# Hybrid decoder trunk: inputs laid out on the host, squares summed on VectorE, a feed-forward entry of four tiles

## The reference

```python
def _rmsnorm(x, g):
    y = xf * lax.rsqrt(jnp.mean(xf * xf, axis=-1, keepdims=True) + NORM_EPS)
    return (y * g.astype(F32)).astype(x.dtype)

def _hybrid_layer(h, ...):
    hn = _rmsnorm(h, g_mix_pre) * valid
    u = (hn @ w_in).astype(F32)                       # 7704 columns, split into the branches
    y_sb, y_gla, y_ml, y_ret = ...                    # stick-breaking, GLA, mLSTM, retention
    gates = jax.nn.sigmoid(merge_logits + b_merge)
    merged = sum(gates[n] * (branches[n] @ w_branch[n]))
    h = h + _rmsnorm(merged @ w_out, g_mix_post)
    f = _rmsnorm(h, g_ffn_pre)
    ffn_out = (jax.nn.silu(f @ ffn_w_gate) * (f @ ffn_w_up)) @ ffn_w_down
    return h + _rmsnorm(ffn_out, g_ffn_post)
```

## Time and profile before

| | us |
|---|---|
| median of 3 runs (lowest, highest) | 961.67 (961.19, 963.05) |
| the profiled execution | 962.09 |
| its span | 959.2 |
| TensorE busy | 947.6 |
| TensorE weight loads busy | 897.3 |
| VectorE busy | 600.6 |
| ScalarE busy | 515.2 |
| GpSimd busy | 80.0 |

### The profile page before, as it was taken

One profiled execution on the slowest core, in us unless ns is written; L12 is line 12 of the kernel. 1 busy time (PEld: TensorE's weight loads), 2 busy tenths in 40 slices (PEclk: granted clock), 3 DMA queues, 4 the chain that ended last, 5 costly groups with the idle time before them and its releaser, 6 DMA issues.

```text
span 959.2 us, 18955 instructions
## 1 busy us (share of the span) xinstructions
PE 947.6 (99%) x7398; PEld 897.3 (94%) x7398; DVE 600.6 (63%) x924; ACT 515.2 (54%) x825; POOL 80.0 (8%) x72
## 2 busy tenths in 40 slices
PE   9999999999999999999999999999999999999998
PEld 7999988899999999999989998988999899999886
DVE  6776675467956655553467775763678666655543
ACT  6645654475466544444456447544854765454442
POOL 1000000000031222210100000000000322221000
PEclk9999999999999999999999999999999999999999
DMA  7585445356553655555545653454564546556652
GB/s 218 171 249 184 147 146 170 124 141 168 174 178 105 196 173 170 172 180 165 166 140 147 211 156 126 134 161 133 141 184 160 176 132 213 181 175 205 211 180 84
DMA packets 165563, 159.41 MB, mean 166 GB/s; under 512 B 9835, under 2 KB 157790, under 8 KB 165502
## 3 DMA queue, kind: packets, MB, share of 16 engines
q1 hardware_dynamic: 163806, 155.17, 52.5%
q10 hardware_dynamic: 1504, 3.33, 1.1%
q0 software_dynamic: 192, 0.07, 0.0%
HBM read 156.37 MB, written 1.06 MB: 164 GB/s over the span
## 4 chain that ended last, share of the span: by engine, by line
PE 94%; DVE 2%; DMA 2%; ACT 1%; SPq 1%; issue 0%; DVEq 0%; ACTq 0%
PE banks L710 25%; PE banks L712 25%; PE banks L711 25%; PE banks L1111 2%; PE banks L1113 2%; PE banks L1112 2%; PE banks L747 2%; PE banks L744 1%; PE banks L743 1%; PE banks L762 1%; DMA raw<-in_w_in 1%; PE banks L976 1%; ACT hi L1195 1%; DVE lo L1610 1%; DMA raw<-in_ffn_w_up 1%; PE banks L974 1%
## 5 line engine op out<-in xcount | busy, mean ns | idle before, releaser
L1610 DVE TENSOR_TENSOR lo<-raw,hi 128x1024 fp32r<-128x1024 f32 (+1 forms) x287 | 347.9, 1216 | 144.9 <-ACT hi L1195 144.3
L710 PE MATMUL banks<-xh,hi 128*128 128x272 f32 (+1 forms) x1456 | 420.1, 289 | 0.2 <-issue 0.2
L712 PE MATMUL banks<-xh,lo 128*128 128x272 f32 (+1 forms) x1456 | 416.3, 286 | 0.0
L711 PE MATMUL banks<-xl,hi 128*128 128x272 f32 (+1 forms) x1456 | 415.0, 285 | 0.0
L1195 ACT ACTIVATE hi<-raw 128x1024 fp32r<-128x1024 f32 (+1 forms) x287 | 300.1, 1048 | 138.5 <-PE banks L712 43.7
L710 PEld LDWEIGHTS banks<-xh,hi 128*128 128x128 f32 x1456 | 274.4, 188 | 6.1 <-issue 4.3
L712 PEld LDWEIGHTS banks<-xh,lo 128*128 128x128 f32 x1456 | 274.5, 189 | 0.0
L711 PEld LDWEIGHTS banks<-xl,hi 128*128 128x128 f32 x1456 | 274.1, 188 | 0.0
L1301 ACT ACTIVATE gates<-banks,par 128x272 f32<-128x272 f32 (+1 forms) x64 | 30.8, 481 | 93.8 <-PE banks L712 91.0
L2114 POOL TENSOR_TENSOR silu_g<-silu_g,rstd 128x272 f32<-128x272 f32 (+1 forms) x44 | 54.5, 1238 | 214.9 <-ACT silu_g L1491 214.9
L2107 POOL TENSOR_TENSOR sq<-sq 128x272 f32<-128x272 f32 (+1 forms) x18 | 21.8, 1213 | 593.0 <-ACT sq L1464 592.1
(11 more groups left out here) (277 smaller groups left out, 1416.1 us busy)
## 6 DMA issues: line engine op xcount, KB each, us to landing
raw<-in_w_in SPq DMA_DIRECT2D x54, 1024.0 KB, 5.3
raw<-in_ffn_w_gate SPq DMA_DIRECT2D x22, 1024.0 KB, 5.3
raw<-in_ffn_w_up SPq DMA_DIRECT2D x22, 1024.0 KB, 5.3
raw<-in_ffn_w_down SPq DMA_DIRECT2D x19, 1024.0 KB, 5.1
raw<-in_w_out SPq DMA_DIRECT2D x8, 1024.0 KB, 5.2
raw<-in_w_in SPq DMA_DIRECT2D x12, 512.0 KB, 4.3
raw<-in_w_branch SPq DMA_DIRECT2D x12, 512.0 KB, 5.5
raw<-in_ffn_w_down SPq DMA_DIRECT2D x4, 768.0 KB, 4.3
```

Source lines behind the costliest of these rows:

```text
L710: mm(dst, wh, mh, start=start, stop=False)
L711: mm(dst, wh, ml, start=False, stop=False)
L712: return mm(dst, wl, mh, start=False, stop=stop)
L1610: tt(half_of(lo, g, c), half_of(raw, g, c), half_of(hi, g, c).bitcast(F32), ALU.subtract).then_inc(lo_ready, 2 if g in G_MIX else 1)
```

## The change

The host now lays out the tokens as `hT` wants them, all parameters as one [128, 2, 88] block, the small group as [128, 8, 128] and the gate weights padded. The transposes, their evictions and the first squares go. Norms 0 and 2 add their squared tiles on VectorE, 8 to 4 to 2, and TensorE takes two. Before the two kinds of boundary (feed-forward entries, entry of layer 1) VectorE makes hi and lo of halves 2 and 3. `together` does all high and low-weight passes of a k step for its tiles before the ones with the low part of x. The feed-forward starts four tiles; layer 1's entry has three tiles in step, and its mean square stands between mqk1's halves.

```diff
-WARM_START, WARM_NORM = 5, 4
-RING, NORM_BANK = (0, 1, 2, 3), 5
+WARM_START, WARM_NORM = 8, 4
+RING, NORM_BANK, INPUT_NORM_BANK = (0, 1, 2, 3), 5, 6
...
-FIRST_LAGS = ((0, KT), (0, 0, 3))
+SUMS = ({0: 2, 1: KT - 2, 2: 2, 3: KT - 2}, {0: 2, 1: KT - 2, 2: 2})
...
+OUT_FIRST, FFN_FIRST, FFN_LATE = 3, 4, 4
+FIRST_ORDER = in_step((0, KT)), [[(n, k) for n in range(3)] for k in range(KT)]
+FFN_ORDER = [[(n, k) for n in range(FFN_FIRST - int(k >= FFN_LATE))] for k in range(KT - 1)]
+FFN_ORDER += [[(n, KT - 1)] for n in range(FFN_FIRST - 1)] + [[(FFN_FIRST - 1, k)] for k in range(FFN_LATE, KT)]
...
 SP:
-            sp.dma_start(xt[0:META, 0, :], meta_tokens).then_inc(meta_loaded, 16)
             for n in range(2):
-                sp.dma_start(xt[:, 1:3, n * 512:n * 512 + 512],
-                             x[0].rearrange("(b p) n -> p b n", p=P)[:, :, n * 512:n * 512 + 512]).then_inc(x_loaded[n], 16)
-            load_rows(sp, PARAM_ROWS[4:7], par_loaded)
+                sp.dma_start(hT[:, 4 * n:4 * n + 4, :], tokens[:, 4 * n:4 * n + 4, :]).then_inc(x_loaded[n], 16)
...
-                        load(g, cols(w_in[l], C_CODE, 32))
-                        sp.dma_start(raw[g % 2][:, :, 32:64], cols(w_in[l], C_MI, 32)).then_inc(small_loaded, 16)
-                        sp.dma_start(raw[g % 2][:, :, 64:128], cols(w_in[l], C_MF, 64)).then_inc(small_loaded, 16)
+                        load(g, w_small[l])
 TensorE, together:
+                for step in steps:
+                    for n, k in step:
+                        ...
+                        if k > high:
+                            high_ready(k)
+                        mm(dst, wh[:, k, f], mh[:, k, q0:], start=k == 0, stop=False)
+                        mm(dst, wl[:, k, f], mh[:, k, q0:], start=False, stop=False)
+                    for n, k in step:
+                        ...
+                        if k > low:
+                            low_ready(k)
+                        last = mm(ps[:, 0:T - q0], wh[:, k, half_cols(g, c)], ml[:, k, q0:], start=False, stop=k == KT - 1)
 TensorE, mean_square:
+                left = (0, KT - 1) if n % 2 else (0, 1)
+                pe.wait_ge(sq_summed[l], sums_before(l, n) + SUMS[l][n])
+                pe.wait_ge(sq_ready[l][n], KT)
+                for k in left:
+                    last = mm(ps[:, 0:T - q0], cut["mean"], sq[:, k, q0:], start=k == 0, stop=k == left[1])
 TensorE, first:
-                    mean_square_first()
                     small_first(t)
-                    together([(t + 1, g + 1, 0), (t + 2, g + 1, 1)], in_step(FIRST_LAGS[l]), uh, ul, 0, *ready)
+                    together([(t + 1, g + 1, 0), (t + 2, g + 1, 1)], FIRST_ORDER[l], uh, ul, 0, *ready)
+                    pe.wait_ge(first_loaded, 16)
+                    mean_square(l, 0, 0)
                 else:
-                    together([(t, g, 0), (t + 1, g + 1, 0), (t + 2, g + 1, 1)], in_step(FIRST_LAGS[l]), uh, ul, 0, *ready,
-                             mean_square(l, 0, 0))
+                    together([(t, g, 0), (t + 1, g + 1, 0), (t + 2, g + 1, 1)], FIRST_ORDER[l], uh, ul, 0, *ready)
 TensorE, group:
+                    if l and name == "mqk1" and j == 0:
+                        mean_square(l, 0, 0)
 TensorE, gate_up:
-                together([(t, g, 0), (t + 1, g, 1), (t + 2, g + 1, 0)], in_step((0, 0, 0)), xh, xl, q0,
-                         lambda k: pe.wait_ge(xh_ready[l], 2 * KT + k + 1), lambda k: pe.wait_ge(xl_ready[l], 2 * KT + k + 1),
-                         mean_square(l, 2, q0))
-                features(t + 3, g + 1, 1, xh, xl, q0)
+                together([(t + n, g + n // 2, n % 2) for n in range(FFN_FIRST)], FFN_ORDER, xh, xl, q0,
+                         lambda k: pe.wait_ge(xh_ready[l], 2 * KT + k + 1), lambda k: pe.wait_ge(xl_ready[l], 2 * KT + k + 1))
+                mean_square(l, 2, q0)
 TensorE, start: the 24 transposes of x and the 2 of the parameters are taken out
 ScalarE, first / output / gate_up / down:
-                for j in range(2):
-                    round_half(half + 2 + j)
+                if l == 0:
+                    for j in range(2):
+                        round_half(half + 2 + j)
...
-                round_half(2 * G_OUT[l] + KT - 2 + ROUND_AHEAD)
                 square_sublayer(l, 1, t + KT - 1, KT - 1, q0)
...
                 for c in range(2):
-                    if c:
-                        round_half(n + 1)
                     gate_tile(c, t + c)
+                round_half(n + 3)
                 for c in range(2):
                     up_tile(c, t + 2 + c, c)
-                    round_half(n + 2 + c)
...
-                        if 2 * j + c < 2 * NDOWN - 1:
+                        if 2 * j + c < 2 * NDOWN - 2:
 ScalarE, order:
+            act.dma_start(par[:], parameters).then_inc(par_loaded, 16)
             act.dma_start(const[:, 0:PIECE_AT[1]], consts[:, 0:PIECE_AT[1]]).then_inc(first_loaded, 16)
...
-                    square_first()
-                    act.wait_ge(bias_loaded, 48)
-                    diagonals()
                     for k in range(KT):
                         round_in(l, k)
-                        if k == 3:
+                    for k in range(KT):
+                        if k == 2:
                             round_half(2)
                             round_half(3)
-                    root(l, 0, 0)
+                        square_h(l, 0, k, 0)
                     round_half(4)
                     round_half(5)
+                    act.wait_ge(first_loaded, 16)
+                    root(l, 0, 0)
                 else:
                     half = 2 * G_MIX[l] + ROUND_AHEAD
-                    round_half(half - 1)
                     for k in range(KT):
                         round_in(l, k)
                         if k == 2:
+                            act.wait_ge(hi_ready, half)
                             round_half(half)
-                    round_half(half + 1)
+                    for n in range(1, 4):
+                        round_half(half + n)
                     root(l, 0, 0)
...
                 root(l, 1, q0)
-                round_half(2 * G_GU[l] - 1 + ROUND_AHEAD)
                 round_ffn_x(l, q0)
-                round_half(2 * G_GU[l] + ROUND_AHEAD)
+                act.wait_ge(hi_ready, 2 * G_GU[l] + ROUND_AHEAD)
+                for n in range(2):
+                    round_half(2 * G_GU[l] + ROUND_AHEAD + n)
                 root(l, 2, q0)
+                round_half(2 * G_GU[l] + ROUND_AHEAD + 2)
 VectorE:
+            def round_and_rest(n):
+                g, c = n // 2, n % 2
+                dve.wait_ge(hi_ready, n)
+                dve.wait_ge(raw_loaded[g % 2], 16 * (g // 2 + 1))
+                dve.wait_ge(half_used, n - 3)
+                nc.vector.tensor_copy(half_of(hi, g, c), half_of(raw, g, c)).then_inc(hi_ready, 1)
+                rest_of_half(n)
+
+            def sum_squares(l, n, q0):
+                ...
+                dve.wait_ge(sq_ready[l][n], KT)
+                tt(sq[:, 0:4, q0:], sq[:, 0:4, q0:], sq[:, 4:8, q0:], ALU.add).then_inc(sq_summed[l], 1)
+                dve.wait_ge(sq_summed[l], done + 1)
+                tt(sq[:, 0:2, q0:], sq[:, 0:2, q0:], sq[:, 2:4, q0:], ALU.add).then_inc(sq_summed[l], 1)
...
 VectorE, rest_of_in and rest_of_ffn_x: no lo inside the k loop any more
 VectorE, first:
+                if l:
+                    pads(l)
+                    rest_of_half(2 * g + REST_AHEAD + 3)
                 dve.wait_ge(rstd_ready[l], 1)
...
 VectorE, gate_up:
+                for ahead in (1, 2):
+                    rest_of_half(n + ahead)
                 dve.wait_ge(rstd_ready[l], 3)
...
                 gate_tile(0, t)
-                rest_of_half(n + 1)
                 gate_tile(1, t + 1)
+                rest_of_half(n + 3)
                 for c in range(2):
                     up_tile(c, t + 2 + c)
-                    rest_of_half(n + 2 + c)
                     rest_of_prod(c, slice(c, c + 1), c + 1)
 VectorE, order:
+            for k in range(2):
                 rest_of_in(0, k)
             scale_small(0, hi_ready)
             scale_small(1, lo_ready)
+            for k in range(2, KT):
+                rest_of_in(0, k)
             rest_of_half(2)
             rest_of_half(3)
+            sum_squares(0, 0, 0)
             for l in range(DEPTH):
                 for n in range(2):
                     rest_of_half(2 * G_MIX[l] + ROUND_AHEAD + n)
+                    if l and n == 0:
+                        sum_squares(l, 0, 0)
                 run_steps(l, parts)
                 output(l)
+                for n in (2, 3):
+                    round_and_rest(2 * G_GU[l] + n)
                 add_sublayer(l, 1, q0, rest_of_ffn_x(l, q0))
+                sum_squares(l, 2, q0)
                 gate_up(l)
                 if l < DEPTH - 1:
                     down(l)
+                    for n in (2, 3):
```

(18 more changed lines are left out.)

214 lines of the change are left out of this document (65 added, 149 removed).

## The result

The changed kernel took 953.86 us (median of 4, 953.76 to 954.93), the kernel before 962.22 (961.19 to 963.05): ratio 0.9921, 95% interval 0.9907 to 0.9934. On another chip it took 954.09 against 961.77: 0.9920 (0.9906 to 0.9933). The forecast was 953.2, in a range of 949.6 to 957.3. The profiled execution took 953.93 us with a span of 951.8; before, 962.09 and 959.2.

A forecast was written before the change was run, and what follows sets the result against it. TensorE was taken to bound the kernel (busy 99%, 94% of the chain of waits). Gains 2.3 + 2.5 + 2.3 + 1.4 = 8.5 us took 962.1 to 953.6 profiled, 953.2 as a median; range 949.6 to 957.3.

The forecast's parts named there:

- Removed passes: Layer 0's feed-forward entry: 2 of 8 mean-square tiles stay, minus 2.8 us; 28 mean-square passes in all.
- The copy at 0.68: Before the boundaries, VectorE's 1024-element SBUF copy of a raw weight half takes 0.68 us; at full length 1.22.
- Layer 0's residual add at 284.57: Layer 0's feed-forward entry: VectorE's copies and low parts, ending at 284.4, stay hidden; the residual add began at 284.57 on rstd.
- half 7: Both feed-forward entries: TensorE, being earlier in its tiles, newly waits 0.7 us for weight half 7.
- Start 2.3: Start: mqk0's weights land at 11.2, first product near 13.7; gain 2.3 us at the gate's bias.
- Entry of layer 1, 2.3: Layer 1's entry: gate at 510.4 instead of 514.0, 3.6 gained, less a new 1.3 bank wait; gain 2.3 us.
- gate-bank wait: Layer 1's entry: gr's second half newly waits 1.3 us for the gate tile's bank, which ScalarE frees behind two halves.
- Layer 1's feed-forward, 1.4: Its entry: VectorE waits for the raw DMA, residual 0.8 later; fifth tile gains 2.1, less 0.7: 1.4 us.
- B: Rival: the new waits at the boundaries don't come, 0.7 + 1.3 + 0.7 us more gained, 950.5; chance 0.20.
- C: Rival: the lower clock comes back as TensorE idles at layer 1's feed-forward entry, costing 2.3 us, 955.5; chance 0.05.
- D: Rival: VectorE's six copies meet GpSimd and take 3.8 us instead of 0.68, 971 to 972; chance 0.04.
- The sign of being wrong: Wrong if the three boundaries' residual adds start more than 1 us later than forecast or the copy takes over 1.3.

The follow-up runs named there:

- e3: Changed kernel, but TensorE sums all eight squares itself at the three later boundaries, VectorE none; 963.65 us against 961.55, ratio 1.0021.
- e6: Changed kernel with the three later boundaries put back and the first post-norm mean-square pass ahead of the last-square wait; 960.85 us, ratio 0.9991.
- c: The changed kernel once more, unchanged, on another chip; 954.09 us against 961.77, ratio 0.9920.
- e4: Changed kernel, but each of VectorE's six copies of a raw half is made twice; 959.77 us against 961.55, ratio 0.9982.
- i6: Changed kernel with four small moves, five GpSimd additions instead of six in layer 1, and its last normalized tile before a waiting rounding; 949.85 us, ratio 0.9875.

## Why the prediction was right

The sum of 8.5 us met 7.4 in the span and 0.8 around it. Most of the second is chance, so the like-for-like gain is 7.5 to 7.7 in this pair and 7.7 to 8.4 in the medians. The mechanism was right. The closeness is in part luck: each of the four stages gave less than forecast (1.9, 2.2, 1.9 and 1.35 for 2.3, 2.5, 2.3 and 1.4), and the chance around the span covers over half of what is missing. By its steps:

- **Removed passes.** Right, and they carry the whole gain (e3). 28 mean-square passes are left. 12.8 us to the fifth tile against a forecast of 13.0, in layer 1 12.1 against 12.3.
- **The copy at 0.68.** Right: 0.68 to 0.70 where no addition of GpSimd was running when it began. The two that began during one took 0.87 and 1.22.
- **Layer 0's residual add at 284.57.** It came at 283.83. The last square is no longer behind a rounding that waits for w_up, so part of the start's gain passes through, and the copies (283.83), not rstd (283.54), end last: the cover that I counted on was short by 0.3 us. With the early start counted apart, this entry gave 3.4 - 0.8 - 0.4 = 2.2 for 2.5; of the 0.4 behind the fifth tile's start half 7 is 0.2.
- **Start 2.3.** 1.9 at the same place (30.66 against 32.52); mqk0's weights landed at 11.65 (2.38 + 9.27 in the chain) instead of 11.2, and the first product came at 14.15 instead of 13.7. The 0.9 "to the semaphore" in that sum is shown by no run: in the trace of before the last packet ended at 12.51 and the landing stands at 12.94, 0.4 later. Other executions had the first product at 14.1 to 15.7, the latest four by the lower clock. The sum put the stages behind it at nothing; 0.4 of the start's 2.0 went there (1.97 to 1.53 at the end of layer 0's output stage). Taken as a term that lasts to the end it was too large: alone it is worth 0.9 (e6).
- **Entry of layer 1, 2.3.** 1.9: the hole grew by 0.51, for the pass behind the last square. This is the step that I missed in all three boundaries: I costed the two passes left and not their order against their wait. The gate-bank wait came as forecast, 1.1 by the waits and 1.2 by the table for 1.3.
- **Layer 1's feed-forward, 1.4.** 1.35 (5.88 to 7.23). First product 4.8 earlier with 5.9 in hand, a loss of 1.1 for the forecast 0.8. The wait that the prediction named didn't come: w_up landed at 751.05, and VectorE, busy with half 1's low part until then, began the copy at 751.58 without idling. That is 0.5 sooner than forecast once the 5.9 are taken off (757.95 - 5.9 = 752.05), but the two pairs took 4.66 us (751.58 to 756.24) instead of 3.82, the rest being what GpSimd's additions held back. The near hit is two errors of opposite sign, luck. Half 7 cost 0.5 for 0.7, in layer 0 0.2.
- **Rivals.** B (no new waits) is out, all three came. C happens in the changed kernel itself, in c and at the start, and cost 0.2 and 0.7 to 0.8 us there and not 2.3; with longer holes it may cost more (e4). D's mechanism is there in small: no copy waited for more than one GpSimd addition.
- **The sign of being wrong.** The residual adds began 0.8, 0.5 and 0.3 us later than forecast when the gain in hand at each is taken off. Read against the sum, in which every earlier stage has given its forecast, they are 1.5 us late each, over the limit of 1 that the prediction set. It didn't say which reading it meant.

## What to carry over

When a pass is removed from a row of passes that wait for different producers, keep each remaining pass behind its own producer only; a joined wait cost 0.5 us a boundary here. Hold the same instruction against itself in both traces at every stage: the differences show at once which stage gave and which hole took back. A start that is early by itself was worth 0.9 of its 2 us here, until places behind it had been moved too. Work that is hidden under a transfer may still matter by keeping TensorE busy; look at the granted clock of the stretch from which it is taken, in more than one profile.

## What the runs showed of the hardware

A VectorE copy that begins while a GpSimd addition runs is longer by a wait for that addition's end, not by a slower rate. With x the time from the copy's start to the addition's end, it took: x 0.32, 0.87 us; 0.47, 1.02; 0.54, 1.09; 0.66, 1.21; 0.72, 1.27, that is x + 0.55 each time; 0.69 for x 0.01 (i6, layer 0), and 0.69 where it came first (the addition starting up to 0.4 us later) or no addition ran. One of the rows (e4, the second copy of a pair):

```profile
485.39 0.94 POOL L2047 TENSOR_TENSOR sq<-sq 128x272 f32<-128x272 f32 x1 [13.39 <-ACT sq L1399]
485.61 1.27 DVE L1559 CAST hi<-raw 128x1024 fp32r<-128x1024 f32 x1
```

The Trainium skill (SBUF — State Buffer, section "SBUF: two separate sides") calls the shared port pair of VectorE and GpSimd an exclusive lock under which the loser fully blocks. The rows agree that it waits; that x + 0.55 is 0.14 less than x and a whole copy of 0.69, they don't explain. Rival D's 3.8 us a copy came nowhere: the longest in all the profiles is 1.27.
